# The last three expert blocks' results summed on the matmul engine, the others gathered sooner, and a third block's rows picked by products

## The reference

```python
def moe(h, w_router, b_router, w_gate, w_up, w_down):   # h: 384 tokens x 1024
    scores = sigmoid(t @ w_router)
    ...                                    # best group of 4 experts, then its best 2
    gates = one_hot(top_idx) weighted by top_w / sum(top_w)
    hidden = silu(einsum('nd,edf->nef', t, w_gate)) * einsum('nd,edf->nef', t, w_up)
    out = einsum('nef,efd->nd', hidden * gates[..., None], w_down)
...
x = x + g2 * moe(h, ...)                   # 16 experts, hidden width 512, two experts per token
```

## Time and profile before

| | us |
|---|---|
| median of 3 runs (lowest, highest) | 1536.72 (1532.25, 1538.74) |
| the profiled execution, its span | 1538.64, 1537.0 |
| PE busy | 1323.6 (86% of the span) |
| DVE, ACT, POOL busy | 520.7, 337.8, 164.4 |
| DMA, mean over the span | 231 GB/s |
| chain that ended last: PE, DMA, DVE, issue, ACT | 65%, 17%, 8%, 7%, 3% |

### The profile page before, as it was taken

One profiled execution on the slowest core, in us unless ns is written; L12 is line 12 of the kernel. 1 busy time (PEld: TensorE's weight loads), 2 busy tenths in 40 slices (PEclk: granted clock), 3 DMA queues, 4 the chain that ended last, 5 costly groups with the idle time before them and its releaser, 6 DMA issues.

```text
span 1537.0 us, 38874 instructions
## 1 busy us (share of the span) xinstructions
PE 1323.6 (86%) x16856; PEld 922.0 (60%) x16856; DVE 520.7 (34%) x1144; ACT 337.8 (22%) x671; POOL 164.4 (11%) x238
## 2 busy tenths in 40 slices
PE   4988899989999989699988669968999878998872
PEld 1447764458888558698544334545664678974441
DVE  1333353135456745011100043458555421111103
ACT  2232211132323122000000033433452300010001
POOL 2013310013343001000000030010000010000001
PEclk9998899999999989899999969988979898999996
DMA  9856436240111163799999981225214477999995
GB/s 396 321 188 218 150 105 260 110 163 6 58 58 58 56 270 152 272 391 385 397 390 413 398 301 65 109 77 214 110 56 165 175 299 266 392 381 401 396 417 191
DMA packets 42106, 354.68 MB, mean 231 GB/s; under 512 B 5708, under 2 KB 10652, under 8 KB 23665
## 3 DMA queue, kind: packets, MB, share of 16 engines
q1 hardware_dynamic: 21456, 302.11, 49.9%
q0 software_dynamic: 8704, 28.53, 5.6%
q10 hardware_dynamic: 11808, 22.03, 4.4%
HBM read 321.63 MB, written 31.01 MB: 229 GB/s over the span
## 4 chain that ended last, share of the span: by engine, by line
PE 65%; DMA 17%; DVE 8%; issue 7%; ACT 3%; POOL 1%; SPq 0%; ACTq 0%; POOLq 0%; DVEq 0%
PE PB L688 59%; DMA ring<-in_w_moe 7%; PE PB L691 6%; DVE arena L2011 3%; DMA arena<-in_w_moe 3%; DMA dispatched<-arena,rows_i 3%; DMA ring<-in_w_mod 2%; ACT arena L1540 1%; DMA arena<-dispatched 1%; DVE small L2024 1%; DMA expert_out<-arena 1%; POOL dispatched L631 1%; DVE arena L2018 1%; DVE arena L2015 1%; DVE x L2011 0%
## 5 line engine op out<-in xcount | busy, mean ns | idle before, releaser
L688 PE MATMUL PB<-arena 64*64 64x64 f32 (+6 forms) x9756 | 495.0, 300 | 52.3 <-DMA arena<-in_w_moe 28.7
L688 PEld LDWEIGHTS PB<-arena 64*64 64x64 f32 (+3 forms) x9756 | 403.8, 131 | 139.2 <-issue 79.2
L688 PE MATMUL PB<-ring,hT 128*128 128x512 f32 (+1 forms) x720 | 313.0, 590 | 7.8 <-DVE hT L2014 3.6
L688 PEld LDWEIGHTS PB<-ring,hT 128*128 128x128 f32 x720 | 136.8, 193 | 166.9 <-issue 161.6
L688 PE MATMUL PB<-ring,arena 128*32 128x256 f32 (+2 forms) x3456 | 202.1, 390 | 22.2 <-DMA ring<-in_w_moe 19.2
L688 PEld LDWEIGHTS PB<-ring,arena 128*32 128x32 f32 x3456 | 150.4, 112 | 65.6 <-DMA ring<-in_w_moe 18.3
L1540 ACT ACTIVATE arena<-PB 128x256 f32<-128x256 f32 (+3 forms) x217 | 106.4, 490 | 339.5 <-PE PB L688 287.4
L691 PE MATMUL PB<-cst,arena 128*128 128x128 f32 (+2 forms) x758 | 117.0, 295 | 65.4 <-DMA arena<-dispatched 26.3
L691 PEld LDWEIGHTS PB<-cst,arena 128*128 128x128 f32 (+2 forms) x758 | 89.8, 155 | 111.2 <-issue 71.8
L2432 DVE TENSOR_TENSOR arena<-arena,PB 128x256 f32<-128x256 f32 (+1 forms) x32 | 15.1, 471 | 302.3 <-PE PB L688 289.1
L688 PE MATMUL PB<-ring,scT 128*32 128x512 f32 x384 | 61.3, 758 | 22.7 <-DMA ring<-in_w_mod 16.8
(11 more groups left out here) (149 smaller groups left out, 925.4 us busy)
## 6 DMA issues: line engine op xcount, KB each, us to landing
arena<-in_w_moe SPq DMA_DIRECT2D x50, 2048.0 KB, 17.5
ring<-in_w_moe SPq DMA_DIRECT2D x46, 2048.0 KB, 15.7
ring<-in_w_mod SPq DMA_DIRECT2D x24, 2048.0 KB, 8.8
ring<-in_w_mix SPq DMA_DIRECT2D x22, 2048.0 KB, 8.3
dispatched<-gate ACTq DMA_DIRECT2D x1, 8320.0 KB, 41.3
arena<-dispatched POOLq DMA_DIRECT2D x20, 256.0 KB, 9.3
expert_out<-gate ACTq DMA_DIRECT2D x1, 3456.0 KB, 15.6
expert_out<-arena ACTq DMA_DIRECT2D x12, 288.0 KB, 9.1
```

The source lines that it names most:

```text
L688: return nc.tensor.matmul(out, lhsT, rhs, start=start, stop=stop, **k)
```

## The change

Block 2's rows are picked by products too, so that PE does block 0's `down` first and then `rows_pick(2)`; POOL's first read of listed rows is block 3's. The jump over the extra blocks moves from behind block 15 to behind block 12's `down` on all engines. Blocks 13, 14 and 15 store nothing: DVE builds for each a matrix (`slotsT`) that holds, for every token and row, the token's weight where the row is the token's; PE turns the three (`spread_T`), ACT and DVE copy them to `spread`, and `combine` on PE adds the three blocks' results, weighted, into six PSUM banks (6 products of 64 rows by 512 columns for each block). The gathers start when block 12's result is stored; a (token, choice) of the last three blocks reads a row of zeros there. `combine_rows` on DVE does with the gathered rows what `combine` did, and the new `combine` adds the PSUM sums. In layer 0 the three modulation chunks come behind all this on PE, one after the other.

```diff
+        spread = take(3 * NTOK).rearrange("p (c n) -> p c n", c=3)
...
+        yg = [hT[:, :].rearrange("p (t d) -> p t d", t=TILES), htok]
+        LAST = NE - 3
...
 # POOL
                 pool.wait_ge(sem("dispatched"), 96 * (l + 1))
-                with pool.Fori(1, FULL // 2) as i:
+                pool.wait_ge(*steps_of(L, "xT_p", None, 1))
+                pool.dma_start(xb[0:CAP, 1, :], Xd[3 * CAP:4 * CAP, :]).then_inc(x_land[1], 16)
+                with pool.Fori(2, FULL // 2) as i:
...
-                pool.wait_ge(*when("y_all", l))
+                pool.wait_ge(*when("extra_done", l))
+                for c in (LAST - 2, LAST - 1):
+                    pool.wait_ge(*stores_of(L, y_st[c % 2], L["stores"][1][c % 2], None, c))
...
 # PE
+            def combine(L, l, c):
+                n, b = c - LAST, c % 2
+                pe.wait_ge(*when("tokens_of", l, n))
+                pe.wait_ge(*steps_of(L, "y_a", None, c))
+                pe.wait_ge(*steps_of(L, "y_v", None, c))
+                for t in range(TILES):
+                    for h in range(2):
+                        r = slice(64 * h, 64 * h + 64)
+                        ins = mm(PB[:, 2 * t + h, :], spread[r, n, 128 * t:128 * t + 128], yb[r, b, 0:512], n == 0, n == 2,
+                                 skip_group_check=True)
+                    ins.then_inc(*tick("pe", "combine", l, n, t))
...
+                        if i is None and c == 1:
+                            down(L, i, 0, 0, CAP)
+                            pe.wait_ge(*steps_of(L, "hT_v", i, 0))
+                            rows_pick(L, l, 2)
...
-                down(L, None, NE - 2, 0, SMALL)
-                hidden_T(L, None, NE - 1, 1, SMALL, 0)
-                down(L, None, NE - 1, 1, SMALL)
                 n_extra = nc.tensor.value_load(xtab[0:1, 31:32], min_val=0, max_val=NX)
+                down(L, None, LAST - 1, 0, SMALL)
                 with pe.If(n_extra > 0):
...
+                rows_T(L, None, LAST + 1, 0)
...
+                pe.wait_ge(*steps_of(L, "xT_v", None, LAST + 2))
+                spread_T(l)
+                gate_up(L, None, LAST + 2, 1, SMALL)
+                hidden_T(L, None, LAST + 2, 1, SMALL, 0)
+                pe.wait_ge(*steps_of(L, "hT_v", None, LAST + 2))
+                for n in range(3):
+                    pe.wait_ge(*when("tokens_of", l, n))
+                combine(L, l, LAST)
+                down(L, None, LAST + 1, 0, SMALL)
+                combine(L, l, LAST + 1)
+                down(L, None, LAST + 2, 1, SMALL)
+                combine(L, l, LAST + 2)
...
 # ACT, behind block 12's store and the jump
+                fn(small[:, 254:255], small[:, 75:76], ACT.Copy, "extra_done", l)
...
+                silu(L, None, LAST + 2, 1, SMALL)
+                for t in range(TILES):
+                    chosen(l, t)
+                y_copy(L, l, LAST + 1)
+                y_copy(L, l, LAST + 2)
...
 # DVE, in route, behind everything the scatter waits for
+                hots_of(2)
+                for n in range(3):
+                    ts(key, rk, float(LAST + n), None, ALU.is_equal, None)
+                    tt(v16(c2[:, 0:48]), v16(picked), bc(key, 1, TILES), ALU.mult)
+                    red(c2[:, 48:51], v16(c2[:, 0:48]))
...
+                    for t in range(TILES):
+                        ts(slotsT[n][:, t, :].rearrange("p (a n) -> p a n", a=2), bc(M("slots")[:, 0:SMALL], 1, 2),
+                           c2[:, 48 + t:49 + t], c2[:, 51 + t:52 + t], ALU.is_equal, ALU.mult,
...
 # DVE, experts: the end
+                hidden_copy(L, None, LAST + 2, 1, SMALL)
+                combine_rows(l, 0)
+                combine_rows(l, 1)
+                out_copy(L, None, LAST + 1, 0, SMALL)
+                combine_rows(l, 2)
+                out_copy(L, None, LAST + 2, 1, SMALL, l)
...
+            def combine(l, t):
+                y1 = yg[1][:, t, :]
+                dve.wait_ge(*when("combine", l, 2, t))
+                tt(y1, PB[:, 2 * t:2 * t + 2, :].rearrange("p b n -> p (b n)"), gatev[:, 0 if t == 0 else 1, 1, :], ALU.mult,
+                   "sum", l, t)
+                tt(xv[:, t, :], xv[:, t, :], y1, ALU.add, "x_moe", l, t)
```

More of the change, by code:

```diff
@@ L465, in experts @@
                 gate_w(L, l, None, 4, 0, e4)
-                with sp.Fori(1, half - 2) as i:
+                with sp.Fori(1, half - 3) as i:
                     es = [expert(bass.ds(i * 2 + n, 1)) for n in (1, 2, 3, 4)]
@@ L507, in _ @@
             experts(0)
-            sp.wait_ge(sem(f"combined{TILES - 1}"), 32)
             for item in stream[first + len(mods_gap):]:
@@ L1842, in experts @@
                     silu(L, None, c + 1, (c + 1) % 2, SMALL)
-                with act.Fori(FULL // 2, half - 1) as i:
+                with act.Fori(FULL // 2, half - 2) as i:
                     for n in (1, 2):
@@ L2461, in experts @@
                     hidden(L, None, c + 1, (c + 1) % 2, SMALL)
-                with dve.Fori(FULL // 2, half - 1) as i:
+                with dve.Fori(FULL // 2, half - 2) as i:
                     for n in (1, 2):
@@ L2480, in experts, with combine_rows @@
                         out_copy(X, i, 0, 0, CAP)
-                if l == 0:
-                    for m, ln in enumerate(mods_gap):
-                        mod_chunk(*ln, 4 + m % 2)
-            def combine(l, t):
+                    dve.wait_ge(*stores_of(X, X["stores"][0][0], X["stores"][1][0], None, NX - 1))
+                rows_copy(L, None, LAST + 1, 0)
+                hidden_copy(L, None, LAST, 1, SMALL)
+                hidden(L, None, LAST + 1, 0, SMALL)
+                rows_copy(L, None, LAST + 2, 1)
+                out_copy(L, None, LAST, 1, SMALL)
+                hidden_copy(L, None, LAST + 1, 0, SMALL)
+                dve.wait_ge(*when("spreadT", l, 1))
+                cp(spread[:, 1, :], PB[:, 2, 0:NTOK], "tokens_of", l, 1)
+                hidden(L, None, LAST + 2, 1, SMALL)
+                hidden_copy(L, None, LAST + 2, 1, SMALL)
[4 more added lines that the diff above has]
+                out_copy(L, None, LAST + 2, 1, SMALL, l)
+            def combine_rows(l, t):
                 dve.wait_ge(*when("chosen0", l, t))
```

189 lines of the change are left out of this document (114 added, 75 removed).

## The result

The changed kernel took 1551.68 us (median of 4 runs, 1544.15 to 1564.84) against 1534.95 for the kernel before: a ratio of 1.0127, 95% interval 1.0088 to 1.0166. Forecast were 1525 and a range up to 1537. Measured again later (e9), the same kernel had 1.0046 (1.002 to 1.0073): still slower, but nearer, and the difference between the two is part of the story.

What follows compares the result with a forecast made beforehand. The weight stream sets the pace, starved at each layer's start while PE waits for rows, with a tail behind the blocks. Layer 1's -13.2 and layer 0's +1.6 give -11.6 us: 1527, 1525 against the median; range 1508 to 1537.

Steps and rivals of the forecast that it cites:

- Term 1: Start of each layer's blocks: block 2's gate starts earlier and the weight stream follows, -9.8 us a layer.
- The rival that the start saves nothing: Layer starts: the stream from 652 on is the bound, the start gains 0 and the tails cost: 1545, chance 0.09.
- Term 2: Gathers beside the weight stream take turns by packets: pairs down at 864, 876, 887 (layer 0) and 1504, 1509, 1512.7 (layer 1).
- the first rival: Gathers beside the weights get half the bandwidth through large packets, down after 17 us: 1514, chance 0.25.
- Term 3: Tail of layer 1: last store ends at 1533.6 against 1537.0, 3.4 us gained, with PE waiting 3.5 us.
- the second rival: Tails of both layers: combine's products do not run side by side, +3.8 and +5.6 us: 1534, chance 0.13.
- Term 4: Tail of layer 0: PE waits some 14 us, then a 20.6 us chain; +1.6 us with term 1's 9.8 taken off.

Runs made afterwards that it cites:

- e9: The changed kernel once more, unchanged, against the kernel before: 1547.16 us, ratio 1.0046.
- e13: The kernel before with only the pick of block 2's rows, tail as before, the same code as e1: 1517.55 us, ratio 0.9872.
- e14: The changed kernel with block 2's rows loaded and transposed as before, only the new tails left, the same code as e2: 1560.76 us, ratio 1.0147.
- e10: The changed kernel with 256 semaphore waits that never wait at the head of TensorE's program: 1542.94 us, ratio 1.0021.
- e7: The changed kernel with POOL issuing the six gathers only when up(15) is done, both layers: 1548.62 us, ratio 1.0052.
- e6: e4, with SP issuing layer 0's three modulation loads only when all six gathers have landed: 1532.51 us, ratio 0.9943.
- e15: The kernel before, unchanged, measured a third time beside e13 and e14: 1540.81 us.
- e3: The changed kernel without the branch for extra blocks on all four engines: 1556.33 us, ratio 1.0113.
- e4: The changed kernel with ACT's and DVE's copies of blocks 14 and 15 ahead of the second pair's work, layer 0 only: 1545.92 us, ratio 1.005.
- e11: e6 with layer 0's modulation chunk copies moved ahead of or between the squares, and layer 1's copies of blocks 14 and 15 moved earlier: 1519.91 us, ratio 0.9879.
- e1: The kernel before with only the pick of block 2's rows, tail as before: 1534.76 us, ratio 0.9987.
- e12: e11 with 256 semaphore waits that never wait at the head of TensorE's program: 1522.39 us, ratio 0.9903.
- e5: The pick alone (e1) with 256 semaphore waits that never wait at the head of TensorE's program: 1525.5 us, ratio 0.9891.
- e2: The changed kernel with block 2's rows loaded and transposed as before, only the new tails left: 1552.68 us, ratio 1.0092.

## Why the prediction was wrong

Two parts of opposite sign, each over 1%, were added up. The experiments separate them: the pick alone is worth -1.28% (e13, -19.7 us on the 1538.64 of that set), the tails alone cost +1.47% (e14, +22.6 us). The forecast had -19.6 and +8.0. So the step that failed is the price of the two tails, terms 3 and 4. The two parts add up to +0.19%, where e10 had +0.21% and e9 +0.46% (0.2% to 0.73%). The run that was forecast lay 0.8% above e9; what of this the gaps explain is told below.

**Term 1 was right, in size too.** Forecast -9.8 us a layer. Without gaps block 2's gate starts 47.2 to 48.2 us behind the first pick instead of 57.0 to 58.1, and the stages of e13 are 21.6 us shorter in sum. The weight stream did follow: in layer 0 the load that takes the place of block 2's gate was issued 53.8 us behind the first pick in e9 and 62.8 in before. A cost of DVE's new operations doesn't show. The rival that the start saves nothing fell. In the first run 5 us a layer were lost again in the dribble, which no row of before shows.

**Term 2, when the gathers land, was right in kind and low in size.** In layer 0 the pairs came at 18.3, 30.7 and 39.3 us, not at 13.7, 25.7 and 36.7. From the first to the second pair it is 12.4 us, 16 rows on each engine, so 0.78 us a turn. The records of the DMA engines agree: in e9, from 858 to 870 us, a 16 KB piece of the weights took 0.62 us and a gathered row of 4 KB 0.16, together 0.78. So the rule of turns holds, and half the bandwidth (17 us for all, the first rival) is out. Of the 4.6 us more for the first pair the records give about half: its first row moved 4.2 us behind the first issue, against 1.7 in before, where the gathers were alone. The rest I can't explain. The term also took it for granted that gathering sooner gains, and worked out only the amount. In layer 0 it gained nothing (e7), with the weights and then three modulation loads on the same engines; those three alone cost the gathers 15 us (e6).

**Term 3, the tail of layer 1: -3.4 forecast, +1.7 measured** (e14 against e15). Without gaps up(15) ends 268.6 to 271.6 us behind the pick with the new tail and 263.4 to 264.4 without it: 4 to 8 us later, where the forecast had 2.5. That reached nothing, since PE had to wait behind it anyway (e3). The combines took 2.85 us, so the second rival is out. Too low was PE's wait, forecast at 3.5 us: in e9 it is 4.73 us, and combine(14) starts 284.4 us behind the pick, by the forecast's times at 279.8. DVE's copy for it stands behind two pairs' work, and the first pair came 5 to 6 us later than I had it: 2.7 of this in e9 because the first gather was issued later, the rest as in term 2. After the wait the 76 records took 8.1 to 8.6 us in e9 and e10 instead of 6.44: the lower clock, which I had charged to layer 0 alone.

**Term 4, the tail of layer 0: +11.4 forecast** (the +1.6 without term 1's 9.8), **+18.9 measured.** The wait was foreseen and its cause too: combine(14) behind ACT's order, "some 14 us", 14.9 in the result. Two sizes were wrong. First, combine(14) began 4.4 us later than forecast in e9, and 9.3 in the first run: the last pair landed 2.6 us later behind the issue, and the first gather was issued 2.1 us (7.0 in the first run) later. Second, the chain behind combine(15): 20.6 us forecast (its three terms give 20.8), 25.6 measured. Four of these five us are the clock's. In e7 the same chain took 21.5 us and its chunks 14.8, as the forecast's 15; in the first run and in e9, where PE was at the clock's lower level under the last chunk (3.64 us for 16 records, 1.92 at full clock), the chunks took 18.1. The forecast had charged the lower clock only to the records right behind the long wait (2.4 us, and 76 records did take 9.2 to 9.4 instead of 6.44), as if the shorter waits between the chunks cost nothing. e4, e6 and e11 took 20.7 us back one after the other by order alone.

So without gaps the changed kernel would still have missed the forecast by 9.9 us in layer 0 and 6.1 in layer 1. The range (up to 1537) left out the case that term 1 holds and the tails cost nearly three times their estimate: I had bounded the gathers from both sides and the chain behind them from none.

**The first run's 0.8% more** is only in part the gaps'. Against e9 they made its two stages 4.6 and 3.9 us longer. By the medians, though, the changed kernel took 4.5 us more than in e9 and the kernel before beside it 5.5 us less (1534.95 against 1540.48), and that second half no profile explains. The gaps stand at two places, up(0) beside the scatter and down(13) beside the gathers, in both layers. The first kind stood in every profile of the first set (e1 to e4) and in the forecast one, the second wherever gathers ran beside the stream there; neither stood in any of the eleven profiles of the later sets, the same programs included. So neither the pick nor the tail nor the place of PE's code brings them by itself. The chip doesn't either: the set with gaps and e9 to e12 ran on the same one. e5's first reading, that the shift had removed them, was an error that e9 and e10 corrected: e5 had no unshifted twin beside it.

**The best version** is the pick alone: 0.9872, 1517.55 us. The repaired tails (e11, 0.9879) draw level with it and don't beat it: the stages of layer 0 are 311.3 us against 308.9. Each was measured in another set without gaps; with them the pick alone had 0.9987.

## What to carry to other kernels

Split a change into its parts before judging it: here a gain of 1.3% and a loss of 1.5% looked like a small loss. Starting a transfer sooner gains only if the DMA engines have room before it is wanted; count what they still have to move, not when the transfer is issued. And where an engine works in order, put the copy that frees TensorE ahead of anything that waits for a DMA: that alone was worth 10 us of layer 0's stage (e4). Waiting costs again afterwards through the clock, after short waits too: 4 us of the chain here. When you read from an engine's row that data came late, look at what stood ahead of it on that engine first, as in e6.

## What the runs showed that I had not expected

The gaps. The starts of the dribbling stretches (608.12, 608.83, 609.55, 610.98) lie 0.71, 0.72 and 1.43 us apart, and one turn of a DMA engine under the full stream was 0.73 to 0.78 us. Instructions come by DMA as well; the page of the profile after lists their queue, with packets of 16 KB:

```profile
q1 hardware_dynamic: 21456, 302.11, 49.3%
q0 software_dynamic: 8480, 27.74, 5.1%
...
q8 instruction: 127, 2.08, 0.5%
```

That PE waited there for instructions, in turns behind weights and rows, would fit both places, which have the scatter or the gathers beside the full stream. The queue's own records speak against it: in the first run its packets start at 600.35 and then at 616.19 us, with none between, and the dribble stands from 606.4 to 611.0.

In the first mixer, where the DMA engines are full in places too, every profile has pauses that no engine is named for, 10.8 us in sum in the first run and 18.2 in e5, whose first pick came latest. Most of the sum is a few long ones; in before one of them is this:

```profile
126.46 1.00 PE L688 MATMUL PB<-arena 64*64 64x64 f32 x13 [5.30 <-issue]
```

So the cause of the dribble is open, and so is why one set has it and the next hasn't. Whether the kernel before had it in the first set is open too, since no profile of it was taken there; its three profiles have none.

What is shown is that one program differs between occasions by more than its interval. e1 and e13 had 0.9987 and 0.9872, with intervals of 0.2% and 0.3% either way. e2 and e14, again one program, had 1.0092 with gaps and 1.0147 without, the other way round: in e2 the wait for the rows hid the gaps at the start, and its stage of layer 0 was 7.0 us shorter, of which 3.6 lie behind combine(15), where PE had the full clock under the last chunk. An interval within one set does not hold such a difference.
